# Local attention in a four-layer encoder: the multiply that normalises the probabilities moves to GpSimd, one of two copies out of PSUM moves to VectorE

## The reference

```
s = (qc @ kb.T) * 64**-0.5
m = max(max(s, axis=-1), sink)            # sink: one learned number per head
p = exp(s - m)
p = p / (sum(p, axis=-1) + exp(sink - m)) # "normalise"
o = (p @ vb) * silu(g)
```

## Time and profile before

| | |
|---|---|
| runs | 1393.66 us median of 3 (1390.51 to 1394.57) |
| profiled execution, own time | 1390.89 us |
| its span | 1389.0 us |
| mean granted TensorE clock | 0.994 of full |
| busy over the whole span | PE 96%, DVE 52%, ACT 31%, POOL 7% |
| the chunk pipeline | 582 to 617 us, 2.5% of the span |

### The profile page before, as it was taken

The page is one execution under the profiler, slowest core; times in us unless marked ns, Lnnn a source line. Parts: engine busy times, 40 slices in busy tenths (PEclk is TensorE's granted clock), DMA queues, the critical chain, the costliest instruction groups (busy, mean ns, idle before and its releaser), DMA issues. The chain is left out here.

```text
span 1389.0 us, 23618 instructions
## 1 busy us (share of the span) xinstructions
PE 1331.2 (96%) x10145; PEld 691.5 (50%) x10145; DVE 716.2 (52%) x1392; ACT 429.9 (31%) x1016; POOL 98.0 (7%) x120
## 2 busy tenths in 40 slices
PE   5999999999999999989999999999999999999998
PEld 3444444478545444564444436544443444468743
DVE  5676776966632011351245013533685875976653
ACT  3124275045212021551212052603112366135401
POOL 0000242010000000000000002000000054010000
PEclk9999999999999999999999999999999999999999
DMA  7221222100600222101322221122422122200231
GB/s 220 76 76 46 76 62 77 30 4 5 246 1 16 76 76 76 62 2 61 78 61 78 78 55 46 45 61 65 141 75 76 47 75 62 61 2 4 75 128 60
DMA packets 111759, 92.45 MB, mean 67 GB/s; under 512 B 5084, under 2 KB 99588, under 8 KB 111144
## 3 DMA queue, kind: packets, MB, share of 16 engines
q1 hardware_dynamic: 110952, 88.82, 21.0%
q10 hardware_dynamic: 704, 2.13, 0.4%
HBM read 84.65 MB, written 6.29 MB: 65 GB/s over the span
## 5 line engine op out<-in xcount | busy, mean ns | idle before, releaser
L1058 PE MATMUL bank<-arena 128*128 128x512 f32 x960 | 420.3, 595 | 1.5 <-ACT arena L645 1.5
L1006 PE MATMUL bank<-arena 64*64 64x64 f32 (+8 forms) x6848 | 316.2, 246 | 14.1 <-issue 3.9
L1058 PEld LDWEIGHTS bank<-arena 128*128 128x128 f32 x960 | 179.9, 190 | 227.8 <-issue 216.3
L1006 PEld LDWEIGHTS bank<-arena 64*64 64x64 f32 (+4 forms) x6848 | 200.4, 133 | 129.4 <-issue 111.3
L168 ACT ACTIVATE arena<-arena 128x512 f32<-128x512 f32 x40 | 25.1, 630 | 221.9 <-DVE arena L989 114.7
L768 DVE SCALAR_TENSOR_TENSOR arena<-arena 128x512 f32<-128x512 f32 x96 | 73.3, 809 | 0.0
L1760 PE MATMUL bank<-arena 128*128 128x512 f32 x160 | 69.2, 593 | 0.6 <-PEq L342 0.6
L671 ACT ACTIVATE arena<-arena 32x128 f32<-32x128 f32 x128 | 54.4, 425 | 37.0 <-DVE arena L790 34.3
L2171 PE MATMUL bank<-arena 128*128 128x512 f32 x128 | 56.2, 593 | 0.9 <-DVE arena L2219 0.9
L351 PE MATMUL bank<-arena 128*128 128x512 f32 x128 | 55.5, 593 | 1.0 <-PEq L1369 1.0
L1390 PE MATMUL bank<-arena 128*128 128x512 f32 x128 | 55.8, 592 | 0.0
(11 more groups left out here) (226 smaller groups left out, 1521.1 us busy)
## 6 DMA issues: line engine op xcount, KB each, us to landing
arena<-in_rw_w_in SPq DMA_DIRECT2D x66, 512.0 KB, 4.1
arena<-in_ml_w_in SPq DMA_DIRECT2D x24, 512.0 KB, 3.8
arena<-in_sw_w_in SPq DMA_DIRECT2D x20, 512.0 KB, 3.8
arena<-in_rw_w_out SPq DMA_DIRECT2D x16, 512.0 KB, 7.2
spill<-arena SPq DMA_DIRECT2D x2, 2048.0 KB, 8.9
arena<-spill SPq DMA_DIRECT2D x2, 2048.0 KB, 13.9
arena<-in_sw_w_out SPq DMA_DIRECT2D x8, 512.0 KB, 3.6
arena<-in_ml_w_out SPq DMA_DIRECT2D x8, 512.0 KB, 3.7
```

The costliest lines, as they stand in the source:

```text
L1006: mm = lambda out, a, b, start=True, stop=True: nc.tensor.matmul(out, a, b, start=start, stop=stop, skip_group_check=True)
L1058: last = nc.tensor.matmul(bank[:, :], slot[:, k, :], mix_at[what][:, k, :], start=k == 0, stop=k == KT - 1)
```

## The change

DVE's `normalise(c)` is split. DVE keeps the sum and the reciprocal (`invert_sums(c)`) and raises a new semaphore, `sums_inverse`; GpSimd, which gets a list of its own, waits for it, makes the 128x1024 multiply and raises `normed`. ACT's `evac(c)` keeps only the copy of the first half. DVE makes the copy of the second half (`evac_second(c)`), which raises a new semaphore, `p_evac_second`. TensorE's `turn` and `outputs` wait for the two semaphores in place of one. DVE's order is written anew. Line numbers in the diff are those of the file before.

```
@@ -1419,7 +1420,8 @@            # turn(c), PE
                     if c >= 1:
-                        pe.wait_ge(p_evac.handle, p_evac.at(2 * c - 1 + q))
+                        evac = (p_evac, p_evac_second)[q]
+                        pe.wait_ge(evac.handle, evac.at(c))
@@ -1433,7 +1435,8 @@            # outputs(c), PE
-                pe.wait_ge(p_evac.handle, p_evac.at(2 * c + 2))
+                pe.wait_ge(p_evac.handle, p_evac.at(c + 1))
+                pe.wait_ge(p_evac_second.handle, p_evac_second.at(c + 1))
@@ -1518,13 +1521,11 @@          # ACT
             def evac(c):
-                for q in range(2):
-                    act.wait_ge(p_turned.handle, p_turned.at(2 * c + q + 1))
-                    if q == 0 and c >= 2:
-                        act.wait_ge(o_done.handle, o_done.at(c - 1))
-                    nc.scalar.activation(pt[c % 2][0:keys(c), 4 * q:4 * q + 4, :], m.bank[4 + q][0:keys(c), :], ACT.Copy)\
-                        .then_inc(p_evac.handle, 1)
+                act.wait_ge(p_turned.handle, p_turned.at(2 * c + 1))
+                if c >= 2:
+                    act.wait_ge(o_done.handle, o_done.at(c - 1))
+                nc.scalar.activation(pt[c % 2][0:keys(c), 0:4, :], m.bank[4][0:keys(c), :], ACT.Copy).then_inc(p_evac.handle, 1)
@@ -1557,6 +1558,14 @@
+        @block.gpsimd
+        def _(pool):
+            for c in range(NC):
+                st, p = small[c % 2], prob[c % 2]
+                pool.wait_ge(sums_inverse.handle, sums_inverse.at(c + 1))
+                nc.gpsimd.tensor_tensor(p[:, :, 0:keys(c)], p[:, :, 0:keys(c)], st[:, 3, :].unsqueeze(2).to_broadcast([P, 8, keys(c)]),
+                                        ALU.mult).then_inc(normed.handle, 1)
@@ -1580,13 +1589,19 @@          # DVE
-            def normalise(c):
-                st, p = small[c % 2], prob[c % 2]
+            def invert_sums(c):
+                st = small[c % 2]
                 dve.wait_ge(s_exp.handle, s_exp.at(c + 1))
                 link(nc.vector.tensor_tensor(st[:, 3, :], st[:, 3, :], st[:, 2, :], ALU.add))
-                link(nc.vector.reciprocal(st[:, 3, :], st[:, 3, :]))
-                nc.vector.tensor_tensor(p[:, :, 0:keys(c)], ...
+                nc.vector.reciprocal(st[:, 3, :], st[:, 3, :]).then_inc(sums_inverse.handle, 1)
+
+            def evac_second(c):
+                dve.wait_ge(p_turned.handle, p_turned.at(2 * c + 2))
+                if c >= 2:
+                    dve.wait_ge(o_done.handle, o_done.at(c - 1))
+                nc.vector.tensor_copy(pt[c % 2][0:keys(c), 4:8, :], m.bank[5][0:keys(c), :].rearrange("p (h k) -> p h k", k=P))\
+                    .then_inc(p_evac_second.handle, 1)
@@ -1615,21 +1630,24 @@          # DVE's order
             maxima(0)
             maxima(1)
-            normalise(0)
-            normalise(1)
+            invert_sums(0)
+            invert_sums(1)
             gate_by_sigmoid(6)
             gate_by_sigmoid(7)
+            evac_second(0)
             maxima(2)
             for c in range(2, NC):
+                evac_second(c - 1)
                 if c + 1 < NC:
                     maxima(c + 1)
-                normalise(c)
+                invert_sums(c)
                 gate(c - 2)
+            evac_second(NC - 1)
             gate(NC - 2)
             gate(NC - 1)
```

More of the change, by code:

```diff
@@ L1363, in sw_layer @@
         "scores_done", "score_max", "scores_exp", "probs_normed", "probs_turned", "probs_evac", "o_done", "o_evac"))
+    p_evac_second, sums_inverse = m.sem("probs_evac_second"), m.sem("sums_inverse")
     m.used_by += [(rows_used.handle, rows_used.at(k + 1)) for k in range(7)] + [(q_done.handle, q_done.at(8))]
@@ L1581, in maxima @@
                 nc.vector.tensor_scalar(st[:, 0, :], st[:, 0, :], -1.0, None, ALU.mult).then_inc(s_max.handle, 1)
-            def normalise(c):
-                st, p = small[c % 2], prob[c % 2]
+            def invert_sums(c):
+                st = small[c % 2]
                 dve.wait_ge(s_exp.handle, s_exp.at(c + 1))
                 link(nc.vector.tensor_tensor(st[:, 3, :], st[:, 3, :], st[:, 2, :], ALU.add))
-                link(nc.vector.reciprocal(st[:, 3, :], st[:, 3, :]))
-                nc.vector.tensor_tensor(p[:, :, 0:keys(c)], p[:, :, 0:keys(c)], st[:, 3, :].unsqueeze(2).to_broadcast([P, 8, keys(c)]),
-                                        ALU.mult).then_inc(normed.handle, 1)
+                nc.vector.reciprocal(st[:, 3, :], st[:, 3, :]).then_inc(sums_inverse.handle, 1)
[5 more added lines that the diff above has]
+                    .then_inc(p_evac_second.handle, 1)
             def gate(c):
@@ L1631, in sw_layer @@
                  (turn_evac, 10), (chain, count[0]), (sink, 64), (rotated, NT), (s_done, NC), (s_max, NC), (s_exp, NC),
-                 (normed, NC), (p_turned, 2 * NC), (p_evac, 2 * NC), (o_done, NC), (o_evac, NC)):
+                 (normed, NC), (p_turned, 2 * NC), (p_evac, NC), (p_evac_second, NC), (sums_inverse, NC), (o_done, NC), (o_evac, NC)):
         s.base += n
```

## The result

1405.82 us (median of 4, 1404.48 to 1407.79), against 1394.06 us for the kernel before (median of 4, with one run more than in the table ahead): ratio 1.010, 95% interval 1.0081 to 1.012. That is 12 us slower; the forecast was 1404.8 us, with a range of 1399 to 1413. In a second set, run beside the first experiments, the same kernel had ratio 1.0079 (1.0065 to 1.0094).

What follows compares the result with a forecast made beforehand. VectorE's sum of work was taken to set the 4.17 us step; a 6.32 us ring would lose 10.0 us and the clock 2.6, together 12.6, giving 1403.5 or 1406.3, said as 1404.8 us, range 1399 to 1413.

Steps and rivals of the forecast that it cites:

- The order closes a ring through VectorE, GpSimd and TensorE: VectorE's new list: the copy waits for turn, turn for GpSimd's multiply, next maxima queue behind; 6.32 us replaces 4.17.
- 6.32 us a round at full clock: From turn to turn: turn 1.09, copy 0.60, maxima 2.00, invert_sums 0.39, multiply 2.04, plus hand-overs; before 4.17.
- The copy, 0.60 on VectorE: evac_second at 128x512, a size with no row: taken as 0.60 us on VectorE, from the gate's time to next start.
- The start: First chunks of the pipeline: maxima(2) stands behind evac_second(0), so turn(2) starts at 592.46 us, not 590.91.
- The clock: three slow turns of six: TensorE's granted clock falls in thinner rounds; a turn costs 1.97 for 1.09, three of six taken, 2.6 us.
- Rival B: The ring without falls of TensorE's clock: +10.0 us, 1400.9 to 1403.7; chance 28%.
- rival C: Lower TensorE clock nearly throughout the pipeline and into the projection: 21.3 us slower, 1412.2 to 1415.0; chance 12%.
- The loss in the layer, 12.6 us: Pipeline to gate(7): 10.0 us from start and longer rounds plus 2.6 from turns at the lower clock.
- my two sums of 1403.5 and 1406.3: Whole kernel: 12.6 us added to the profiled execution's 1390.89, and to the runs' median, 2.8 above it.
- VectorE's wait at the copy, 2.7 us: VectorE reaches evac_second(c) 0.60 us after invert_sums, the turn ends 3.33 after: a wait of 2.7 per chunk.
- Rival A: Engine loads count: VectorE needs 3.63 us per chunk, not 4.17, so 3.2 us gained, 1387.7 to 1390.5; chance 2%.
- All at one for one: Behind the layer: what the pipeline loses, the program loses in full; nothing later hides it.

Runs made afterwards that it cites:

- the first trace: Profile of the changed kernel, unaltered, from its first timed set: 48.41 us from scores(2) to the projection's first product, against 35.04 before; timed ratio 1.010.
- the changed kernel's second trace: Profile of the same changed kernel, unaltered, run again beside the first experiments: 47.1 us from scores(2) to the projection's first product; ratio to before 1.0079.
- the order without the ring: Changed kernel with only VectorE's list re-ordered, copy of chunk c-1 behind maxima(c+1) and invert_sums(c): ratio 0.9995 to the kernel before.

## Why the prediction was right

- **The order closes a ring through VectorE, GpSimd and TensorE.** Right, and shown: opening it by order alone takes the whole loss away with GpSimd in it, and without GpSimd all but the 0.60 us a chunk by which VectorE's work grows. Each of maxima (2.00) and an added multiply (1.0) is paid as it leaves or enters it.
- **6.32 us a round at full clock.** Measured 6.16. The term off is the multiply, 1.90 for my 2.04; with it the sum is 6.18. The rest is the hand-over to VectorE, 0.04 for my 0.07. (Half of the figure of the Trainium skill, "GPSIMD Engine Reference", section "Elementwise — side-by-side cycle accounting", was 2.25 us, an estimate from that page, and too long by more than my value from the rows. My remark that the rows at 512 columns are quicker than that rate, 1.12 us for 512, holds for the 1.04 but not for the 1.22.)
- **The copy, 0.60 on VectorE.** Measured 0.61 to the next start (610.10 to 610.71), where it follows a wait.
- **The start.** turn(2) was forecast 10.38 us after scores(2) (592.46 - 582.08); it came 10.33 after in both traces.
- **The clock: three slow turns of six.** In the first trace five of the turns (2) to (7) were slow, two of them not in full, in the second two and a part. That makes 4.2 and 2.4 us, and my 2.6 lay between; 0.88 each was right, three was a guess. Rival B, no fall, did not occur in either trace. The lower clock did not reach the projection's products in either, so rival C fell.
- **The loss in the layer, 12.6 us.** 13.4 and 12.1 in two traces. Two misses cancel in part: the ring alone costs 9.2 us, an estimate from the measured start and rounds at full clock, not 10.0, and the clock took 4.2 in one trace and 2.9 in the other, not 2.6 (the 2.9 holds 0.5 for outputs at the lower clock in front of turn(7), which I had put at nothing). That the median came within 1 us of 1404.8, a value between my two sums of 1403.5 and 1406.3, is in part luck.
- **VectorE's wait at the copy, 2.7 us.** 3.43 with a turn of 1.92, and 2.60 in the changed kernel's second trace where the turn took 1.09; the shorter multiply makes the difference.
- **Rival A, the loads.** Fell as forecast; but also in the order without the ring the promised 3 us did not come. There my picture, VectorE's sum as the step, was too simple: the ring over two chunks, through turn, outputs, scores, maxima and the multiply, sets 3.88 us a chunk.
- **All at one for one.** Nothing behind the layer took up the loss: the part behind it was 1.8 us longer in the first trace, not shorter.

## What to carry to other kernels

When work is moved to another engine, look at the lists before the loads: which entry now waits for something that the same engine released a moment earlier, and what is queued behind it. Here a copy out of PSUM, put ahead of the next chunk's maxima, closed a ring and cost 11 us; one or two places further down it cost nothing. A loop's step is the larger of the fullest engine's work and the longest ring, where a ring that goes around once in two chunks counts half (7.77 us made a step of 3.88). A short sum over the ring, hand-overs included, gave the step of the changed kernel to 3%.

## What was not expected of the hardware

The time outside the touched stage moves by some us from run to run: scores(2), which stands behind code that is nearly the same in all kernels, started at 581.2 to 585.7 us in twelve profiles, and two short falls of the granted clock (to 0.50, near 1254 and 1340 us) stood in one profile of the changed kernel, one or none in others. So a difference of one profiled execution, 17.0 us here, can be 5 us off the median's 11.8.

GpSimd's multiply of twice the columns took 1.90 us against 1.04 (line 611 in the earlier trace rows, and the same 1.04 for this multiply in chunk 0, which has 512 columns), so 0.86 for 512 more columns; and it took the same 1.90 whether VectorE was waiting or was copying, gating and reducing from banks beside it.
